# Query latents and pool inputs of a hybrid decoder's front stage as four pairs of seven half products; one memory query feature moves into the front stage

## The reference

```python
h = rms_norm(x, attn_norm)                       # 576 x 2048
z = h @ w_in                                     # to 5,376 columns
q_a, ckv, krope, u, qm, gate = split(z)          # 512, 256, 64, 512, 512, 2048 + ...
q = rms_norm(q_a) @ w_q_b                        # latent attention (MLA), 8 heads
pool = (windowed mean(u) - u) @ w_pool * scale   # windows 2, 4, 8, 16; state of 15 rows
mk, mv = rms_norm(mem) @ w_mem_kv                # memory keys and values of the prompt
mix = concat[mla, pool, cross(qm, mk, mv)] * silu(gate)
y = rms_norm(x + mix @ w_out)
```

## Time and profile before

| What | Value |
|---|---|
| time, median of 3 runs | 867.82 us (867.19 to 867.97) |
| the profiled execution's span | 865.3 us |
| TensorE busy | 856.4 us, 99% of the span |
| VectorE, ScalarE, GpSimd busy | 590.4, 464.5, 147.4 us |
| granted TensorE clock, mean | 0.997 |
| DMA | 168.56 MB, 195 GB/s over the span |

### The profile page before, as it was taken

The page is one execution under the profiler, slowest core; times in us unless marked ns, Lnnn a source line. Parts: engine busy times, 40 slices in busy tenths (PEclk is TensorE's granted clock), DMA queues, the critical chain, the costliest instruction groups (busy, mean ns, idle before and its releaser), DMA issues.

```text
span 865.3 us, 15858 instructions
## 1 busy us (share of the span) xinstructions
PE 856.4 (99%) x5549; PEld 781.2 (90%) x5549; DVE 590.4 (68%) x1018; ACT 464.5 (54%) x774; POOL 147.4 (17%) x210
## 2 busy tenths in 40 slices
PE   9999999999999999999999999999999999999996
PEld 9999999999989999999999999888887788888885
DVE  6546635532349688888888875967678889563777
ACT  7665422122233566676667663577777546363446
POOL 0003001411300112323232331000000111111123
PEclk9999999999999999999999999999999999999998
DMA  9895435223364587878788754524127775988586
GB/s 357 303 290 208 134 134 182 73 85 103 102 256 182 175 275 245 253 256 248 250 254 251 250 172 136 220 86 159 37 97 299 165 213 115 257 218 262 118 156 218
DMA packets 64878, 168.56 MB, mean 195 GB/s; under 512 B 9672, under 2 KB 27657, under 8 KB 62808
## 3 DMA queue, kind: packets, MB, share of 16 engines
q1 hardware_dynamic: 52672, 126.46, 42.4%
q0 software_dynamic: 10752, 33.56, 16.9%
q10 hardware_dynamic: 1376, 7.54, 2.5%
HBM read 156.14 MB, written 11.50 MB: 194 GB/s over the span
## 4 chain that ended last, share of the span: by engine, by line
PE 99%; ACT 0%; issue 0%; DVE 0%; POOL 0%; ACTq 0%; DVEq 0%; POOLq 0%
PE z L67 8%; PE z L69 8%; PE z L68 8%; PE z_acc L67 6%; PE z_acc L68 6%; PE z_acc L69 6%; PE pa_s L67 4%; PE pa_s L69 4%; PE pa_s L68 4%; PE pa_qk L69 3%; PE pa_qk L68 3%; PE pa_qk L67 3%; PE kv_acc L67 3%; PE kv_acc L68 3%; PE kv_acc L69 3%; PE ps_s L1431 2%
## 5 line engine op out<-in xcount | busy, mean ns | idle before, releaser
L67 PE MATMUL z<-x_hi,w_hi 128*128 128x288 f32 x512 | 152.5, 298 | 0.0
L69 PE MATMUL z<-x_hi,w_lo 128*128 128x288 f32 x512 | 150.8, 294 | 0.0
L68 PE MATMUL z<-x_lo,w_hi 128*128 128x288 f32 x512 | 150.7, 294 | 0.0
L184 ACT ACTIVATE w_hi<-w_raw 128x1024 fp32r<-128x1024 f32 (+2 forms) x62 | 64.8, 1045 | 135.7 <-PE z L69 55.0
L191 DVE TENSOR_TENSOR w_lo<-w_raw,w_hi 128x1024 fp32r<-128x1024 f32 (+2 forms) x62 | 76.9, 1241 | 70.8 <-ACT w_hi L184 70.4
L1024 POOL DMA_DIRECT2D v_raw<-in_cache x128 | 69.3, 541 | 176.0 <-issue 174.4
L67 PEld LDWEIGHTS z<-x_hi,w_hi 128*128 128x128 f32 x512 | 96.1, 188 | 2.7 <-issue 1.1
L68 PEld LDWEIGHTS z<-x_lo,w_hi 128*128 128x128 f32 x512 | 96.1, 188 | 1.6 <-issue 0.2
L69 PEld LDWEIGHTS z<-x_hi,w_lo 128*128 128x128 f32 x512 | 96.0, 188 | 0.0
L2056 ACT ACTIVATE o_hi<-o_raw 128x1024 fp32r<-128x1024 f32 x50 | 52.9, 1060 | 71.1 <-PE pa_s L3030 38.1
L2310 DVE TENSOR_TENSOR o_lo<-o_raw,o_hi 128x1024 fp32r<-128x1024 f32 x50 | 60.9, 1220 | 34.6 <-ACT o_hi L2056 34.4
(11 more groups left out here) (551 smaller groups left out, 2406.8 us busy)
## 6 DMA issues: line engine op xcount, KB each, us to landing
w_raw<-in_w_feat SPq DMA_DIRECT2D x56, 512.0 KB, 4.0
k_raw<-in_cache SPq DMA_DIRECT2D x128, 192.0 KB, 3.1
v_raw<-in_cache POOLq DMA_DIRECT2D x128, 128.0 KB, 3.3
o_raw<-in_w_out POOLq DMA_DIRECT2D x30, 512.0 KB, 8.4
o_raw<-in_w_out SPq DMA_DIRECT2D x20, 512.0 KB, 8.5
w_raw<-in_w_mem_kv SPq DMA_DIRECT2D x16, 512.0 KB, 4.3
gate_spill<-gate_tmp SPq DMA_DIRECT2D x16, 288.0 KB, 3.3
mix<-gate_spill SPq DMA_DIRECT2D x4, 1152.0 KB, 10.3
```

The lines of the kernel that those rows point to most:

```text
L67: pe.matmul(out, a[0], b[0], start=start, stop=False, skip_group_check=onto)
L68: pe.matmul(out, a[0], b[1], start=False, stop=False, skip_group_check=onto)
L69: return pe.matmul(out, a[1], b[0], start=False, stop=stop, skip_group_check=onto)
L184: act.activation(hi_slot(s, u)[:, lo:w], s.wraw[:, u % RAW, lo:w], ACT.Copy).then_inc(s.w_hi, 1)
```

## The change

The eight tiles of the query latents (four) and of the pool inputs (four) are no longer made one by one. They are taken as four pairs of tiles. For a pair, the weights are four blocks a, b, c, d (two tiles by two halves of the 2048 rows), x is four blocks (two halves of the rows by two halves of the 576 columns), and the four block results are made from seven products of blocks of 8 x 288 (Winograd's form of Strassen's scheme) instead of eight. Each of the products has 8 x 3 = 24 matmuls of 288 columns.

- `w_pair` holds the weight blocks, 16 loads of 512 KB. A pair has eight slots; roles rotate among them. The sums of weight blocks are X = c + d and Y = X - a (VectorE, `first`, `second`), c := a - c and Z = b - Y (GpSimd, `third`, `fourth`).
- The differences of blocks of x are made once: `fs` is x scaled by the gain, by GpSimd for the row blocks 0 to 12 (`ACT_F` = 13), by ScalarE for the rest; three differences by VectorE, one by GpSimd (`traw`), each 128 x 2304; the high parts by ScalarE (`turned_hi`), the low ones by VectorE (`turned_lo`).
- The 28 products stand directly behind the latents; ScalarE copies three partial sums of a pair out of PSUM, VectorE adds six (288 columns each). The scaling by 1/rms follows later, for all four latents in one instruction, and for each pool input in `finish_u`.
- Behind the products comes a new order of memory units and feature halves (`ORDER`): four gates and, last in the front, one memory query feature, whose sum VectorE takes out at the start of the middle stage.
- The memory tokens, pool state and tables are loaded behind product 21. Tiles of the front get new places in SBUF, some of them in turn.
- The middle has 60 parts instead of 64, and `LONG` is 2, 4, 8, 10, 14, 16, 20, 22, 26 and the last step.

```diff
-UU, QA, PGATE, GATE, QM = range(0, 4), (4, 5, 6, 11), range(7, 11), range(12, 24), range(24, 28)
-FEATS, FRONT = 28, 12
+PGATE, GATE, QM = range(0, 4), range(5, 17), (4, 17, 18, 19)
+FEATS, FRONT = 20, 5
+ORDER = [("f", 0), ("f", 1), ("m", 0), ("m", 1), ("m", 2), ("m", 3)]
+for n_ in range(2, 8):
+    ORDER += [("f", n_), ("m", 2 * n_), ("m", 2 * n_ + 1)]
+ORDER += [("f", 8), ("f", 9)]
+PAIRS, TERMS = 4, 7
+TERM_ROLE = "XYZcadb"
...
         @block.gpsimd
+            for c, (k0, k1) in enumerate(X_CHUNKS):
+                pool.wait_ge(xt_landed[c], 16)
+                for k in range(k0, min(k1, ACT_F)):
+                    pool.tensor_scalar(fs[:, 2 * (k // 8):2 * (k // 8) + 2, k % 8, :], halves(xraw[:, k, :]), gx[:, k:k + 1], None,
+                                       ALU.mult).then_inc(scaled, 1)
+            def third(n):
+                pool.wait_ge(s12, 2 * n + 1)
+                pool.wait_ge(ab_in, 32 * (n + 1))
+                pool.tensor_tensor(raw(n, "c"), raw(n, "a"), raw(n, "c"), ALU.subtract).then_inc(s3, 1)
...
+            pool.wait_ge(scaled, ACT_F)
+            pool.wait_ge(x_hi, 2 * KD - ACT_F)
+            pool.wait_ge(x_lo, KD)
+            pool.tensor_tensor(traw[:, 2, :, :], fs[:, 3, :, :], fs[:, 1, :, :], ALU.subtract).then_inc(s3, 1)
+            fourth(0)
+            third(0)
+            for n in range(1, PAIRS):
+                third(n)
+                fourth(n)
...
         @block.scalar
+            for k in range(ACT_F, KD):
+                act.activation(fs[:, 2:4, k % 8, :], halves(xraw[:, k, :]), ACT.Identity, scale=gx[:, k:k + 1]).then_inc(x_hi, 1)
+            turned_hi(1)
+            pair_hi(0)
+            square_row(0)
+            turned_hi(2)
+            pair_hi(1)
+            turned_hi(3)
+            pair_hi(2)
+            turned_hi(4)
...
         @block.vector
+                if k == 12:
+                    dve.wait_ge(scaled, 8)
+                    dve.tensor_tensor(traw[:, 0, :, :], fs[:, 1, :, :], fs[:, 0, :, :], ALU.subtract).then_inc(t_sum, 1)
+            dve.wait_ge(scaled, ACT_F)
+            dve.wait_ge(x_hi, 2 * KD - ACT_F)
+            dve.tensor_tensor(traw[:, 1, :, :], fs[:, 3, :, :], traw[:, 0, :, :], ALU.subtract).then_inc(t_sum, 1)
+            first(0)
+            turned_lo(1)
+            second(0)
+            pair_lo(0)
+            dve.tensor_tensor(traw[:, 3, :, :], fs[:, 2, :, :], traw[:, 1, :, :], ALU.subtract).then_inc(t_sum, 1)
+            turned_lo(2)
+            pair_lo(1)
+            pair_lo(2)
+            turned_lo(3)
+            for step in range(PRODUCTS):
...
+                if i == 4 and n_ + 1 < PAIRS:
+                    second(n_ + 1)
+                if step + HI < PRODUCTS:
+                    pair_lo(step + HI)
...
+                if i == 3 and n_ + 1 < PAIRS:
+                    first(n_ + 1)
+                if step == 1:
+                    turned_lo(4)
...
         @block.tensor
+            def pair_product(m):
+                n, i = divmod(m, TERMS)
+                turned = {0: 1, 1: 2, 3: 3, 5: 4}
...
+                pe.wait_ge(st_hi, hi_count(m))
+                pe.wait_ge(st_lo, lo_count(m))
+                w = high(s, m % HI), low(n, TERM_ROLE[i])
+                for kk in range(8):
+                    last = product(pe, sums_bank(n, bank), [v[:, P * kk:P * kk + P] for v in w],
+                                   (b[0][:, kk, :], b[1][:, kk, :]), start and kk == 0, kk == 7, not start)
+                last.then_inc(s.st_used, 1)
+            for m in range(PRODUCTS):
+                pair_product(m)
...
-LONG = (*range(2, 28, 2), STEPS - 1)
+LONG = (2, 4, 8, 10, 14, 16, 20, 22, 26, STEPS - 1)
```

More of the change, by code:

```diff
@@ L352, in _ @@
             sp.wait_ge(out, 16 * (6 + DB))
+            for i in range(GT):
+                sp.wait_ge(s.spilled[i], 16 * len(range(i, GR, GT)))
             sp.wait_ge(s.stored[0], 32)
@@ L377, in _ @@
[L377 to L389 removed]
+                pool.wait_ge(u_ready, 3 * (g + 1))
@@ L498, in _ @@
[L498 to L511 removed]
+                if j in BEND_AT:
+                    g = BEND_AT[j]
+                    act.wait_ge(z_out, g + 1)
@@ L532, in m_link, with first, second @@
                 dve.wait_ge(m_chain, l[0])
+            def first(n):
+                dve.wait_ge(cd_in, 32 * (n + 1))
+                if n == 0:
+                    dve.wait_ge(s.w_used, 3)
+                else:
+                    dve.wait_ge(s.st_used, TERMS * (n - 1) + 4)
+                dve.tensor_tensor(raw(n, "X"), raw(n, "c"), raw(n, "d"), ALU.add).then_inc(s12, 1)
+            def second(n):
+                dve.wait_ge(s12, 2 * n + 1)
+                dve.wait_ge(ab_in, 32 * (n + 1))
+                if n == 0:
+                    dve.wait_ge(s.w_used, 4)
+                else:
+                    dve.wait_ge(s.st_used, TERMS * (n - 1) + 5)
+                dve.tensor_tensor(raw(n, "Y"), raw(n, "X"), raw(n, "a"), ALU.subtract).then_inc(s12, 1)
@@ new lines, in pair_lo @@
+            def pair_lo(m):
+                n, i = divmod(m, TERMS)
+                role = TERM_ROLE[i]
+                dve.wait_ge(st_hi, hi_count(m))
+                if role in "Xa":
+                    dve.wait_ge(s12, 2 * n + 2)
+                if role == "a":
+                    dve.wait_ge(s3, n + 2)
+                if role == "d":
+                    dve.wait_ge(s12, 2 * n + 1)
+                if role in "Yb":
+                    dve.wait_ge(s4, n + 1)
+                dve.tensor_tensor(low(n, role), raw(n, role), f32(high(s, m % HI)), ALU.subtract).then_inc(st_lo, 1)
@@ L723, in _ @@
             for _ in range(WARM):
-                pe.matmul(z[:, 0, 0, 0:P], s.ones[:], s.ones[:], start=True, stop=True)
+                pe.matmul(ps[:, 0, 0:P], s.ones[:], s.ones[:], start=True, stop=True)
             for u in range(KV_UNITS):
                 latents(u)
-            for i in range(MIXED):
-                memory(2 * i)
-                if i == 2:
+            for m in range(PRODUCTS):
+                pair_product(m)
+                if m == 12:
                     pe.wait_ge(diag, TT)
-                    zf = k4[:, 2:4, :].rearrange("p a b -> p (a b)")
+                    pe.wait_ge(kv_raw, TT)
+                    zf = ps[:, 6:8, :].rearrange("p a b -> p (a b)")
@@ L3287, in laid_out @@
     feats = [None] * FEATS
-    for start, which in ((0, QA), (o, UU), (o + MW, QM)):
-        for i, j in enumerate(which):
-            feats[j] = w[:, start + P * i:start + P * i + P]
+    for i, j in enumerate(QM):
+        feats[j] = w[:, o + MW + P * i:o + MW + P * i + P]
+    paired = [w[:, start + P * i:start + P * i + P] for start in (0, o) for i in range(4)]
+    w_pair = np.stack(paired).reshape(PAIRS, 2, 2, 8, P, P).transpose(0, 1, 2, 4, 3, 5).reshape(PAIRS, 4, P, 8 * P)
     o += 2 * MW
```

774 lines of the change are left out of this document (472 added, 302 removed).

## The result

The changed kernel takes 892.41 us (median of 4, 892.24 to 893.03) beside 867.76 for the kernel before: ratio 1.0287, interval 1.0273 to 1.0302, so 24.6 us slower. The forecast was slower, by 9.6 us, and its range ended at 886: the time lies above it. The profiled execution spans 890.5 us, 25.2 more than before. One execution of the later run fixes2_scale13, 1393.18 us at a granted clock of 0.557, was in a slow state and is left out of its median and ratio.

What follows compares the result with a forecast made beforehand. TensorE was taken to bound the kernel, busy 856.4 of 865.3 us. Products 22.4 us late less 12.8 saved gave +9.6 us on the 867.8 median: 877.4 us, range 857 to 886.

Steps and rivals of the forecast that it cites:

- The saving: TensorE: 16 half units, 102.2 us, become 28 products of 24 matmuls, 89.5 us; 12.8 us saved.
- The lateness of the products: Product 5 starts at 76.0 instead of 55.6, 20.4 us late; with 2.0 added over products 5 to 10, 22.4.
- GpSimd's differences: Up to product 5, one block difference (3.8 us) and two weight differences (1.85 each) exclude VectorE, 7.5 us in all.
- The scalings at 0.95 us each: Front: each of GpSimd's 13 scalings of x excludes VectorE for 0.95 us, 12.4 in all; bounds 0 and 1.55.
- Products 5 to 10 and later: VectorE and GpSimd owe 16.6 us against TensorE's 16.0, 2.0 added; later 17 of 22.4 us a pair, lateness unchanged.
- The clock: Behind product 0's wait, the first product or two may run at 1.2 GHz, 0 to 3.2 us each; range only.
- nothing later on is waited for: Behind product 10 the lateness stays what it is, and nothing gives it back.
- The middle: Middle stage: loses four fill parts of 3.2 us, the rest still covers the vector work; 0, up to 2 us lost.
- The case in which GpSimd's work hides in gaps: Front: GpSimd's work falls into VectorE's gaps and costs TensorE nothing; 9.3 us faster, 858.5 us; chance 17%.
- the one in which scalings exclude nothing: Front: only the two-input differences exclude VectorE; 12.4 us less than the forecast, 865.0 us; chance 17%.
- The case in which they exclude for all their time: Front: GpSimd's scalings exclude VectorE for their whole length, 13 x 0.6 us more, 885.2 us; chance 20%.
- (1): Sign: TensorE idle some 16 us between the last latent matmul (about 40 to 43 us) and the first half product.

Runs made afterwards that it cites:

- fixes2_scale13: Changed kernel with all fixes together and their order mended, but 13 scalings on GpSimd instead of 8: 871.85 us, ratio 1.0043 to the kernel before.
- all_vector: Changed kernel with GpSimd's block difference and eight weight differences made by VectorE; GpSimd keeps the 13 scalings: 881.29 us, ratio 1.0162.
- scale8: Changed kernel with GpSimd scaling 8 of the 16 input blocks instead of 13, ScalarE the other 8: 889.90 us, ratio 1.0247.
- early_sum: Changed kernel with VectorE making the first two weight sums ahead of the second block difference: 888.38 us, ratio 1.0233.
- warm_wait: Changed kernel with TensorE filling its first two waits with matmuls of ones whose sums nobody reads: 890.72 us, ratio 1.0270.
- gate_order: Changed kernel with GpSimd's two gate products of group 0 ahead of group 3's windows instead of behind them: 882.07 us, ratio 1.0153.
- all_fixes3: Changed kernel with all fixes together, their order mended, 8 scalings on GpSimd, and the squares of the rows respaced: 867.29 us, ratio 0.9995.
- fixes3_warm: all_fixes3 with 26 filling matmuls of ones in TensorE's wait between products 0 and 1: 866.96 us, ratio 0.9995.
- t3_vector: Changed kernel with GpSimd's one block difference of 2304 elements made by VectorE, behind the first low part: 889.92 us, ratio 1.0247.

## Why the prediction was right or wrong

**The saving** was right: 3.176 us a product against 3.195, 13.3 us against 12.8.

**The lateness of the products** was right in size, 24.1 us at product 26 against 22.4, and partly by luck, for its terms were wrong in both directions:
- *Which product decides.* I added up VectorE's work to product 5. But product 5 waited for nothing. Product 1 was 15.8 us late (59.03 against 43.3), and 1.6 of half clock makes the 17.3 of product 5, where I had 20.4. VectorE's own work alone would have had product 1's operands ready at 46.3 by my own figures, 3.0 us late. On top came 9.3 us held by GpSimd's differences, 2.0 by its scalings and 1.0 of wait for the 13th of them: 58.6, and the low part ended at 58.9.
- *VectorE's own work:* 2.55 and 1.22 us an instruction, as priced. When VectorE makes every difference itself (all_vector), product 26 is still 13.7 us late, and after the reordering 134.14 - 123.7 = 10.4; but then its work holds nine differences more than in the changed kernel.
- *The scalings at 0.95 us each* (12.4 in all): mis-sized. They made VectorE's low parts of x 0.33 us longer each and its queue 2.0 us late in all. What they cost besides was GpSimd's own pace, 2.27 us each, so that the 13th ended at 34.7 and the second difference waited for it. Fewer of them gained 3.5 us (scale8).
- *GpSimd's differences:* 4.9 us for the large one against 3.8, 2.2 for each small one against 1.85: 9.3 against 7.5. Here the lock between the engines is as forecast, and as the Trainium skill ("SBUF — State Buffer", section "SBUF: two separate sides") has it. The scalings by a column would by that page hold VectorE as fully. There the traces differ: one took 1.8 us where VectorE had little to do (3.54 us for the first two in early_sum) and held a low part of x back by 0.33, a weight's low part of 960 and a block difference of 2304 not at all.
- *Products 5 to 10 and later:* 6.8 us came behind product 5 against my 2.0. I took the later pairs as covered because the two engines' work fitted into TensorE's time. It fitted on average; GpSimd weight differences fell just on low parts that TensorE needed next. Waits at products 7, 14 and 21 make 5.0 of it (1.98, 0.76 and 2.27), the lower clock at product 7 another 1.6.
- *The clock*, left out of the sum: 1.6 us each at products 1 and 7, of which warm_wait gave back the first. The longest stretch at the lower clock, product 0's, lay ahead of a wait and cost nothing.

**The step that failed** is "nothing later on is waited for", with its companion that the memory units cost 0 to 2 us. The second stall took 8.25 us of idle time and 2.6 of half clock; gate_order gave 11.6 us back with one move. I counted VectorE's and GpSimd's work and the slots of the memory units, but didn't walk through GpSimd's program in order. It has the gate products of all groups behind the windows of all groups, as before; and in the diff both `DIFF_AT` and `BEND_AT` have an entry at unit 16, so that there ScalarE waits for a product that stands behind the last windows, and these for VectorE's differences at that same unit. Without this stall the result is about 881 (gate_order), inside the range and near the forecast of 877.4.

**The middle** lost 2.3 us, a little over the 0 to 2 allowed; 1.4 of them are short waits of the score matmuls for the low and high parts of the keys.

**The rivals.** The case in which GpSimd's work hides in gaps (858.5) and the one in which scalings exclude nothing (865.0) both failed, though the scalings nearly excluded nothing: GpSimd's pace, the two-input differences and the waits in the later pairs took the place. The case in which they exclude for all their time (885.2) lies nearest to the time measured, and that is chance: its mechanism is the one that the 0.33 us refute. Of the list of signs, (1), (3), (5) and (6) showed, (1) with 10.4 us of wait for 16; (2) and (4) half, since the 13th scaling ended at 34.7, ahead of the 38 to 48, and 2.1 us of wait came as late as product 21; (7) did not. Of the three things that were to prove it wrong, the last came true: the memory units stalled by over 2 us, and the middle by 2.3.

The delays separate: about 11 us from the order in GpSimd's program, about 11 from two-input work on GpSimd instead of VectorE, and some 10 to 14 that stay at product 26 when both are mended. Against these stand 13.3 saved. The first two are shown by runs and can be had back. Of the third, 10.4 us in all_fixes3, 6.6 stand ahead of product 1 (49.93), where VectorE works without a wait from 31.16 on; 2.7 are product 1's half clock (5.89 us for 3.18) and 0.8 the wait at product 7. Of these only the half clock was taken away (fixes3_warm), and then ScalarE's queue held the next operands; a run with the row's square out of its way there was not made. With all of it mended the change is worth nothing, 867.29 against 867.36. Whether a product whose input needs no difference could go first was not tried.

## What to carry to other kernels

Where a change trades matmuls for sums, walk each engine's program in order through the new stage, not only its hours: one wait in front of a queue of unrelated work cost nearly as much here as the whole saving. Give GpSimd no two-input work beside a full VectorE: the block difference that it took over held VectorE 4.9 us, and VectorE makes it in 2.55. And ask which product the time hangs on: in t3_vector the first started 4.9 us earlier, but the second only 2.4 and the last ones 1.5.

## What was not expected of the hardware

GpSimd's scaling by a column (576 elements) made VectorE's `scalar_tensor_tensor` of 576 0.33 us longer and left its `tensor_tensor` of 960 and of 2304 elements as they were, at 1.14 and 2.55 us, where GpSimd's two-input differences held VectorE whole, 2.2 us for 1024 elements and 4.9 for 2304. Why is open.

The granted clock was still 0.99 in the 3.1 us of idle time from 55.94 to 59.03, then 0.50 in the 3 us behind it: the loss shows behind the wait, not in it. And behind a wait of 1.8 us product 7 ran at 0.64 in one trace and at 1.00 in another.
